# The delta rule's chunks and its output norm as one written-out stage, with two kinds of masked factors made by GpSimd

## The chip, the cores and the metric

One Trainium2 chip, one of its cores. The metric is the device time of one execution of the whole program in microseconds (us), the median of several runs. The engines are named as in the profile: PE is TensorE (PEld its weight loads), DVE is VectorE, ACT is ScalarE, POOL is GpSimd, SP the queue that issues the DMAs.

## What is computed

The program is two models in a row, on 512 tokens of width 1024 in float32: a block of differential attention, a state-space scan and a mixture of 64 experts, and then two layers, each of which mixes tokens in three ways (a delta rule with decay, a retention and a latent attention) before a gated feed-forward. The change is in the delta rule of these two layers. Its reference, cut to the recurrence and the norm after it (4 heads of 64):

```python
def step(state, inp):
    rt, kt, vt, wt, kkt, at = inp
    sa = jnp.einsum('bhvk,bhk->bhv', state, -kkt)
    state = (state * wt[:, :, None, :] + sa[..., None] * (kkt * at)[:, :, None, :]
             + vt[..., None] * kt[:, :, None, :])
    return state, jnp.einsum('bhvk,bhk->bhv', state, rt)
...
mean = jnp.mean(y, axis=-1, keepdims=True)
var = jnp.mean(jnp.square(y - mean), axis=-1, keepdims=True)
y = ((y - mean) * lax.rsqrt(var + RW_GN_EPS)).reshape(B, S, RW_DIM) * gn_w + gn_b
bonus = jnp.sum(r_h * k_h * r_k, axis=-1, keepdims=True) * v_h
y = (y + bonus.reshape(B, S, RW_DIM)) * g
```

## The kernel before

The program is a row of stages. Each stage is one block of five instruction streams, in the order in which they are written, which hand work to each other by semaphores; all engines meet at a barrier at its end. Nothing of one stage runs beside another.

The recurrence is done in chunks of 64 tokens. A tile `t` (there are NT = 4) holds two chunks on its 128 partitions and the 4 heads side by side, so that most tiles are 128 x 512. `stage_rwkv_chunks` has these steps:

- **Products** (L2915 to L2931 on PE, L3031 to L3043 on DVE, L3009 to L3013 on ACT). For each `t`, five products of 4 matmuls with a drain after each. DVE multiplies each by a mask from PSUM into SBUF (LT, Ti, MT, RB, RK) and then makes the first factors: `Ti = ident - Ti` (L3040), `TT = ident - LT * level0` (L3041, L3043). Six transposes per `t` go to ACT.
- **Inversion** (L2933 to L2956, L3014 to L3018, L3045 to L3061). Five levels in a hardware loop (`Fori`), each over the 4 tiles, that is 20 units `u`. For a unit DVE makes the masked factor `Lm = LT * level mask` (L3050), PE does `first`, 4 matmuls of Lm and Ti (L2952), ACT copies the result to X (L3018), PE does `second`, 4 matmuls to update Ti (L2942) and 4 to update TT (L2943), and DVE subtracts them (L3059, L3060). A float32 matmul is two passes in the trace, so a unit has 8 + 16 passes. On PE, `second` of a tile follows `first` of the next; `first` of every tile waits for `t_new` of the whole level before (L2949), and the factor of the next level is made after the last update of this one.
- **Mixed values and weighing** (L2958 to L2971): 4 matmuls of MT and the values per tile, 4 of TT and AM per tile, all after the last level; DVE copies the result into TW.
- **Parts** (L2973 to L2990). For each `t` 12 matmuls (the "front": G and y) and then 24 small ones of 64 x 64 (the "back": H and Z), one drain. Then DVE takes all of them (L3070 to L3081: one subtraction, one copy, 8 small instructions for H, 2 copies for Z). PE waits for `gh` of this tile before it begins the next (L2976).
- **States** (L2992 to L2996, L3083): 7 steps in a chain, PE then DVE. **Outputs** (L2998 to L3005, L3086): 4 tiles, PE then DVE.

`stage_rwkv_out` (L3095) is the norm of y over each head, on DVE alone but for one square root on ACT: 13 instructions, 10 of them over all 1024 columns, with a drain after each. `second_layer` calls both (L3173 to L3176) between `stage_mix` and `stage_ffn`, once in each layer.

Of the kernel before, what the change touches and what calls it, by code (L numbers as in the profile page):

```python
# [17 lines left out]
ds = bass.ds  # L18
# [2862 lines left out]
def stage_rwkv_chunks(k, l, out, eb, vt, y, spent):  # L2881

# [9 lines left out]
    W4 = HH * P  # L2892
    with ExitStack() as ctx:
# [10 lines left out]
        S = k.sb(f"rc{l}_S", [P, 8, 2, CH], F32, ctx)  # L2904
        bk = k.banks(ctx, 8, f"rc{l}_bk")
        lane = lambda h: slice(64 * (h % 2), 64 * (h % 2) + 64)
        pair = lambda p: (2 * (p % 3), 2 * (p % 3) + 1)
        s_ = {n: k.sem(f"rc{l}_" + n) for n in ("prod", "masked", "turned", "tok_taken", "lm", "x_mm", "x_sb", "y_mm", "t_new", "mv", "am", "tw_mm", "tw",
                                               "gh_mm", "gh", "s_mm", "s_new", "yo_mm", "yo_taken", "zero")}
        with nc.Block() as block:  # L2910
            @block.tensor
            def _(pe):
                pe.sem_inc(s_["y_mm"], 2)

                for t in range(NT):  # L2915
                    sl = slice(t * P, (t + 1) * P)
                    for n, (lhs, rhs) in enumerate(((B_, A_), (A_, B_), (K_, A_), (B_, R_), (K_, R_))):
                        if 5 * t + n >= 3:
                            pe.wait_ge(s_["masked"], 5 * t + n - 2)
                        for h in range(HH):  # L2920

                            o = bk[pair(5 * t + n)[h % 2]][:, (h // 2) * P:(h // 2 + 1) * P]
                            ins = pe.matmul(o, lhs[lane(h), h // 2, sl], rhs[lane(h), h // 2, sl], start=True, stop=True)
                        pe.drain().then_inc(s_["prod"], 1)
                    if t:
                        pe.wait_ge(s_["tok_taken"], 2 * t)
                    for n, src in enumerate((A_, Be, Ke)):
                        for b in range(2):
                            o = n * RW + b * P
                            ins = pe.transpose(bk[6 + o // 512][:, o % 512:o % 512 + P], src[:, b, sl], k.c("ident"))  # L2930
                    ins.then_inc(s_["turned"], 1)  # L2931

                pe.wait_ge(s_["masked"], 5 * NT)  # L2933
                with pe.Fori(0, 5) as lv:
                    def second(t):

                        u = lv * 4 + t
                        pe.wait_ge(s_["x_sb"], u + 1)
                        pe.wait_ge(s_["t_new"], u + 1)
                        for h in range(HH):  # L2940
                            hs = slice(h * P, (h + 1) * P)
                            pe.matmul(bk[2 + t % 2][:, hs], TT[:, t, h, :], X[t % 2][:, hs], start=True, stop=True)  # L2942
                            ins = pe.matmul(bk[4 + t % 2][:, hs], X[t % 2][:, hs], TT[:, t, h, :], start=True, stop=True)  # L2943
                        ins.then_inc(s_["y_mm"], 1)

                    for t in range(NT):
                        u = lv * 4 + t
                        pe.wait_ge(s_["lm"], u + 1)
                        pe.wait_ge(s_["t_new"], lv * 4 + 2)  # L2949
                        for h in range(HH):  # L2950
                            hs = slice(h * P, (h + 1) * P)
                            ins = pe.matmul(bk[t % 2][:, hs], Lm[t % 2][:, hs], Ti[:, t, h, :], start=True, stop=True)  # L2952
                        ins.then_inc(s_["x_mm"], 1)
                        if t:
                            second(t - 1)
                    second(NT - 1)  # L2956

                pe.wait_ge(s_["t_new"], 2 + 5 * NT)  # L2958
                for t in range(NT):
                    if t >= 2:  # L2960
                        pe.wait_ge(s_["am"], t - 1)
                    for h in range(HH):
                        ins = pe.matmul(bk[t % 2][:, h * 64:h * 64 + 64], MT[:, t, h, :], vt[:, t, h * 64:h * 64 + 64], start=True, stop=True)
                    ins.then_inc(s_["mv"], 1)
                for t in range(NT):
                    pe.wait_ge(s_["am"], t + 1)
                    if t >= 2:
                        pe.wait_ge(s_["tw"], t - 1)
                    for h in range(HH):
                        ins = pe.matmul(bk[2 + t % 2][:, h * P:(h + 1) * P], TT[:, t, h, :], AM[:, t, h, :], start=True, stop=True)  # L2970
                    ins.then_inc(s_["tw_mm"], 1)  # L2971

                for t in range(NT):  # L2973
                    pe.wait_ge(s_["tw"], t + 1)
                    if t:
                        pe.wait_ge(s_["gh"], t)  # L2976
# [15 lines left out]
                for c in range(7):  # L2992
                    pe.wait_ge(s_["s_new"], c + 1)
                    for h in range(HH):
                        ins = pe.matmul(bk[c % 2][lane(h), (h // 2) * 64:(h // 2) * 64 + 64], H[lane(h), h // 2, c, :], S[lane(h), c, h // 2, :], start=True, stop=True)
# [506 lines left out]
```

## Time and profile before

| | us |
|---|---|
| runs of the program | 3936.82, 3932.77, 3932.19 (median 3932.77) |
| profiled execution | 3927.36 |
| its span in the profile | 3925.5 |
| PE, DVE, ACT, POOL busy in the span | 3311.0, 1511.0, 1098.5, 175.8 |
| the two stages of layer 0 | 2347.8 to 2537.4 on the span's clock |
| the two stages of layer 1 | 3281.0 to 3472.3 |

A row of the timeline gives start, duration, engine, line, operation, output<-inputs, shape and count, and in brackets how long the engine was idle before it and for whom. PEq and DVEq are the engines' own sequencers: a wait for a drain of PE or DVE. A duration of a row with several instructions is from the first start to the last end. The granted clock of PE has two levels, 2.4 GHz (1.00) and 1.2 GHz (0.50).

### The profile page before, as it was taken

How to read it: one execution, taken by the hardware profiler on the slowest of the kernel's cores; microseconds unless marked ns; L12 is line 12 of the kernel's file. 1: busy time of each engine (PE TensorE's matmuls, PEld its weight loads, DVE VectorE, ACT ScalarE, POOL GpSimd, SP SyncE). 2: the span in 40 equal slices, each digit the busy share in tenths (PEclk: the TensorE clock that was granted, in tenths of full speed). 3: DMA queues.
4: the chain of work that ended last, by engine and by line, in shares of the span. 5: the costliest groups of instructions: out<-in, count | busy, mean ns of one | idle time of the engine just before them, and what ended most of it. 6: DMA issues, size and time to landing. Idle time of an engine off the chain costs nothing. (4 is left out here: it accounts for less than half of the span.)

```text
span 3925.5 us, 42592 instructions
## 1 busy us (share of the span) xinstructions
PE 3311.0 (84%) x16382; PEld 2352.5 (60%) x16382; DVE 1511.0 (38%) x2518; ACT 1098.5 (28%) x1853; POOL 175.8 (4%) x204
## 2 busy tenths in 40 slices
PE   5998999999677788787849888599998988769997
PEld 3776877777333233333317557478886746757886
DVE  4772566643410001000034565433323665443332
ACT  3672666642100000000013341132223242123221
POOL 0000222200000000000000000000000000000000
PEclk9999999999799999989979978599999986779999
DMA  3223222223899999999943100123323100022332
GB/s 93 64 66 67 71 65 65 65 70 95 327 427 426 426 426 425 416 415 421 415 184 93 28 1 1 35 78 97 99 97 83 49 11 1 1 78 81 97 102 76
DMA packets 355521, 601.90 MB, mean 153 GB/s; under 512 B 72288, under 2 KB 306560, under 8 KB 330624
## 3 DMA queue, kind: packets, MB, share of 16 engines
q1 hardware_dynamic: 346112, 590.85, 41.2%
q0 software_dynamic: 9216, 8.42, 0.6%
q8 instruction: 128, 2.10, 0.2%
q14 instruction: 65, 0.53, 0.0%
HBM read 603.40 MB, written 20.97 MB: 159 GB/s over the span
## 5 line engine op out<-in xcount | busy, mean ns | idle before, releaser
L1729 PE MATMUL ex_up<-ex_W,ex_XT 128*64 128x512 f32 x1024 | 262.2, 670 | 97.0 <-DMA ex_W<-in_w_expert_up_dram 97.0
L226 ACT ACTIVATE f_hi<-f_raw 128x1024 fp32r<-128x1024 f32 x148 | 156.8, 1059 | 576.0 <-PE ff_bk L286 548.8
L1729 PE MATMUL ex_gp<-ex_W,ex_XT 128*64 128x512 f32 x1024 | 237.8, 618 | 59.7 <-DMA ex_W<-in_w_expert_gate_dram 58.3
L235 DVE TENSOR_TENSOR f_lo<-f_raw,f_hi 128x1024 fp32r<-128x1024 f32 x148 | 181.1, 1224 | 257.9 <-ACT f_hi L226 257.7
L284 PE MATMUL ff_bk<-h_a_hi,f_hi 128*128 128x512 f32 x704 | 275.9, 392 | 2.8 <-DVE h_a_lo L3361 2.8
L285 PE MATMUL ff_bk<-h_a_lo,f_hi 128*128 128x512 f32 x704 | 275.3, 391 | 0.0
L286 PE MATMUL ff_bk<-h_a_hi,f_lo 128*128 128x512 f32 x704 | 275.1, 391 | 0.0
L1772 DVE TENSOR_TENSOR ex_hid<-ex_sg,ex_up 128x512 f32<-128x512 f32 x32 | 22.0, 688 | 614.9 <-PE ex_up L1729 614.9
L1758 PE MATMUL ex_yp<-ex_W,ex_hT 128*64 128x512 f32 x1024 | 226.8, 594 | 35.1 <-DMA ex_W<-in_w_expert_down_dram 20.3
L1729 PEld LDWEIGHTS ex_up<-ex_W,ex_XT 128*64 128x64 f32 x1024 | 92.3, 153 | 266.3 <-issue 266.3
L1729 PEld LDWEIGHTS ex_gp<-ex_W,ex_XT 128*64 128x64 f32 x1024 | 87.6, 142 | 209.0 <-issue 207.2
L235 DVE TENSOR_TENSOR b_lo<-b_raw,b_hi 128x1024 fp32r<-128x1024 f32 (+1 forms) x121 | 147.9, 1234 | 124.0 <-ACT b_hi L226 123.8
L284 PE MATMUL ff_bk<-f_hi,fT_hi 128*128 128x512 f32 x480 | 187.6, 391 | 0.0
L285 PE MATMUL ff_bk<-f_lo,fT_hi 128*128 128x512 f32 x480 | 187.1, 390 | 0.0
L286 PE MATMUL ff_bk<-f_hi,fT_lo 128*128 128x512 f32 x480 | 187.0, 390 | 0.0
L1758 PEld LDWEIGHTS ex_yp<-ex_W,ex_hT 128*64 128x64 f32 x1024 | 84.7, 137 | 155.2 <-issue 155.2
L284 PE MATMUL ss_acc<-h_x_hi,b_hi 128*128 128x512 f32 x320 | 131.9, 412 | 29.3 <-DVE b_lo L235 29.3
L226 ACT ACTIVATE b_hi<-b_raw 128x1024 fp32r<-128x1024 f32 (+1 forms) x121 | 125.7, 1048 | 109.9 <-PE mg_bk L286 64.9
L284 PEld LDWEIGHTS ff_bk<-h_a_hi,f_hi 128*128 128x128 f32 x704 | 133.0, 189 | 31.6 <-DVE h_a_lo L3361 3.6
L286 PEld LDWEIGHTS ff_bk<-h_a_hi,f_lo 128*128 128x128 f32 x704 | 133.0, 189 | 27.8
L285 PEld LDWEIGHTS ff_bk<-h_a_lo,f_hi 128*128 128x128 f32 x704 | 133.1, 189 | 27.5
L286 PE MATMUL ss_acc<-h_x_hi,b_lo 128*128 128x512 f32 x320 | 128.6, 402 | 0.0
(606 smaller groups left out, 6620.4 us busy)
## 6 DMA issues: line engine op xcount, KB each, us to landing
ex_W<-in_w_expert_gate_dram SPq DMA_DIRECT2D x64, 2048.0 KB, 29.4
ex_W<-in_w_expert_up_dram SPq DMA_DIRECT2D x64, 2048.0 KB, 29.6
ex_W<-in_w_expert_down_dram SPq DMA_DIRECT2D x64, 2048.0 KB, 28.9
b_raw<-in_w_in_dram SPq DMA_DIRECT2D x88, 512.0 KB, 3.9
f_raw<-in_w_gate_up_dram SPq DMA_DIRECT2D x88, 512.0 KB, 3.8
f_raw<-in_w_down_dram SPq DMA_DIRECT2D x44, 512.0 KB, 3.5
m_raw<-in_w_in_dram SPq DMA_DIRECT2D x40, 512.0 KB, 4.0
b_raw<-in_w_branch_ssd_dram SPq DMA_DIRECT2D x16, 512.0 KB, 4.0
```

The costliest lines, as they stand in the source:

```text
L226: a.activation(self.hi[n % self.SLOTS][:, at], self.raw[n % self.RAW][:, at], ACT.Copy).then_inc(self.cast, 1)
L235: v.tensor_tensor(self.lo[i][:, at], self.raw[n % self.RAW][:, at], self.hi[i][:, at].bitcast(F32), ALU.subtract).then_inc(self.split_done, 1)
L284: pe.matmul(out, a[0], b[0], start=first, stop=False)
L285: pe.matmul(out, a[0], b[1], start=False, stop=False)
L286: return pe.matmul(out, a[1], b[0], start=False, stop=last)
L1729: ins = pe.matmul(ps[part[e], :], XT[b][:, q, part[e]], row_view(slots[e], KD)[:, q, :], start=(q == 0), stop=(q == KD - 1))
L1758: ins = pe.matmul(y_ps[s][part[e], :], hT[:, q, part[e]], row_view(slots[e], HT)[:, q, s * 512:(s + 1) * 512], start=(q == 0), stop=(q == ...
L1772: v.tensor_tensor(hid[:], sg[:], u_ps[:], ALU.mult).then_inc(hid_ready, 1)
```

## The change

The two stages become one, `stage_delta`. What it does:

- The level loop is written out over 20 units. `first(u)` waits for the factor `lm` of this unit and for `t_new` of the same tile one level before. In the last level the update of Ti is left out.
- GpSimd makes the first TT factors (two instructions per tile) and all 20 `Lm`. It then makes `eye` and `H = pc * eye`, and the norm's `gate` and `gt` with four instructions of 128 x 1024.
- Mixed values run on PE behind units 0 to 3, weighing behind the last units. ACT takes TW, y and Z in place of DVE.
- In the parts, front and back have their own drain and semaphores, and nothing waits for the taking of the same tile. States 1 to 3 and the outputs are placed between and behind the parts, the norm is done per tile, between the later states. State 0 is a copy.
- y, gate, sq and the norm's rows lie in memory left by an earlier stage. The norm's rows are loaded at the stage's begin.

The diff, cut to its core:

```diff
-                with pe.Fori(0, 5) as lv:
...
+            @block.gpsimd
+            def _(g):
+                for t in range(NT):
+                    g.wait_ge(masked, 5 * t + 1)
+                    g.tensor_tensor(TT[:, t], LT[:, t], over("rw_level0"), ALU.mult)
+                    g.drain()
+                    g.tensor_tensor(TT[:, t], over("ident"), TT[:, t], ALU.subtract).then_inc(tt_ready, 1)
+                for u in range(LEVELS * NT):
+                    t = u % NT
+                    if u >= 2:
+                        g.wait_ge(x_mm, u - 1)
+                    g.tensor_tensor(Lm[t % 2][:].rearrange("p (h n) -> p h n", h=HH), LT[:, t], over(f"rw_level{u // NT + 1}"), ALU.mult).then_inc(lm, 1)
...
+            @block.tensor
+                def first(u):
+                    t = u % NT
+                    pe.wait_ge(lm, u + 1)
+                    if u < NT:
+                        pe.wait_ge(ti_ready, t + 1)
+                    else:
+                        pe.wait_ge(t_new, u - NT + 1)
+                    if u >= 2:
+                        pe.wait_ge(x_sb, u - 1)
...
+                def parts(t):
+                    pe.wait_ge(tw, t + 1)
                     if t:
+                        pe.wait_ge(front_v, t)
+                        pe.wait_ge(front_a, t)
...
+                    pe.drain().then_inc(front_mm, 1)
+                    if t:
+                        pe.wait_ge(back_v, t)
+                        pe.wait_ge(back_a, t)
...
+                first(0)
+                for u in range(1, LEVELS * NT):
+                    first(u)
+                    second(u - 1)
+                    if u <= NT:
+                        mixed_values(u - 1)
+                    if u >= LAST + 2:
+                        weigh(u - LAST - 2)
+                second(LEVELS * NT - 1)
+                weigh(NT - 2)
+                weigh(NT - 1)
+                parts(0)
+                parts(1)
+                state(1)
+                parts(2)
+                state(2)
+                parts(3)
+                state(3)
+                outputs(0)
+                state(4)
+                outputs(1)
+                state(5)
+                outputs(2)
+                state(6)
+                outputs(3)
...
+            @block.vector
+                def spread(t):
+                    v.drain()
+                    do(v.tensor_reduce, mean[:, t, :], heads(y, t), AX, ALU.add)
+                    do(v.tensor_scalar, mean[:, t, :], mean[:, t, :], 1.0 / 64, None, ALU.mult)
+                    do(v.tensor_tensor, heads(y, t), heads(y, t), each(mean, t), ALU.subtract)
+                    do(v.tensor_tensor, sq[:, t, :], y[:, t, :], y[:, t, :], ALU.mult)
+                    do(v.tensor_reduce, var[:, t, :], heads(sq, t), AX, ALU.add)
+                    v.tensor_scalar(var[:, t, :], var[:, t, :], 1.0 / 64, 64e-5, ALU.mult, ALU.add).then_inc(var_ready, 1)
+                def normalize(t):
+                    v.wait_ge(root_ready, t + 1)
+                    do(v.reciprocal, var[:, t, :], var[:, t, :])
+                    do(v.tensor_tensor, heads(y, t), heads(y, t), each(var, t), ALU.mult)
+                    if t == 0:
+                        v.wait_ge(gates_ready, 1)
+                    do(v.tensor_tensor, y[:, t, :], y[:, t, :], gt[:, t, :], ALU.mult)
+                    v.tensor_tensor(mix[:, t, 0:RW], y[:, t, :], gate[:, t, :], ALU.add)
...
+                for u in range(LEVELS * NT):
+                    update(u)
+                take_front(0)
...
+                take_back(3)
+                add_state(3)
+                add_outputs(0)
+                add_state(4)
+                spread(0)
+                add_outputs(1)
+                add_state(5)
+                normalize(0)
+                add_outputs(2)
+                add_state(6)
+                spread(1)
+                spread(2)
+                normalize(1)
+                add_outputs(3)
+                spread(3)
+                normalize(2)
+                normalize(3)
```

## Rows read from the trace of the kernel before

**Rows 1.** Windows of the two stages: us, PE, PEld, DVE, ACT, POOL busy, clock, DMA, GB/s.

```profile
2347.80:2381.80 34.00, 30.42 (x184) 23.28 (x184) 22.97 (x53) 3.49 (x8) 0.00 (x0) 0.50 0.00 1
2381.80:2462.40 80.60, 67.24 (x544) 66.07 (x544) 41.35 (x66) 15.00 (x28) 0.00 (x0) 0.93 0.00 0
2462.40:2471.20 8.80, 5.60 (x73) 4.47 (x72) 3.79 (x14) 0.00 (x0) 0.00 (x0) 1.00 0.01 2
2471.20:2507.60 36.40, 28.34 (x216) 22.49 (x216) 7.14 (x26) 0.00 (x0) 0.00 (x0) 0.50 0.00 1
2507.60:2537.40 29.80, 7.66 (x120) 5.61 (x120) 20.22 (x40) 1.50 (x2) 0.00 (x0) 0.50 0.03 9
...
3313.40:3397.30 83.90, 70.64 (x544) 69.50 (x544) 41.36 (x66) 15.02 (x28) 0.00 (x0) 0.90 0.00 0
```

**Rows 2.** Timeline, end of the products and begin of the inversion, both layers.

```profile
2373.37 0.75 DVE L3035 TENSOR_TENSOR rc_LT<-rc_bk,more_consts 128x256 f32<-128x256 f32 x2
...
2379.51 0.63 PE L2930 MATMUL rc_bk<-consts,rw_Ke 128*128 128x128 f32 x2
...
2382.71 3.57 PE L2952 MATMUL rc_bk<-rc_Ti,rc_Lm 128*128 128x128 f32 x16 [2.57 <-DVE rc_Lm L3050]
...
3310.68 0.38 PE L2930 MATMUL rc_bk<-consts,rw_Ke 128*128 128x128 f32 x2
...
3314.30 1.52 PE L2952 MATMUL rc_bk<-rc_Ti,rc_Lm 128*128 128x128 f32 x5 [3.24 <-DVE rc_Lm L3050]
```

**Rows 3.** Timeline inside the inversion, two units and the next level's begin.

```profile
2388.11 0.69 DVE L3059 TENSOR_TENSOR rc_Ti<-rc_Ti,rc_bk 128x512 f32<-128x512 f32 x1 [2.60 <-PE rc_bk L2943]
...
2390.79 0.69 DVE L3059 TENSOR_TENSOR rc_Ti<-rc_Ti,rc_bk 128x512 f32<-128x512 f32 x1 [0.51 <-PE rc_bk L2943]
...
2397.98 2.05 PE L2952 MATMUL rc_bk<-rc_Ti,rc_Lm 128*128 128x128 f32 x16 [2.76 <-DVE rc_Lm L3050]
```

**Rows 4.** Timeline, mixed values and weighing of layer 0.

```profile
2454.79 3.79 PE L2963 MATMUL rc_bk<-rw_vt,rc_MT 128*128 128x64 f32 x32 [1.41 <-DVEq L3061]
2458.41 4.10 PE L2970 MATMUL rc_bk<-rc_AM,rc_TT 128*128 128x128 f32 x32
```

**Rows 5.** GpSimd's instructions of two lines, min/median/max in ns.

```profile
L883 POOL TENSOR_TENSOR ss_rows<-consts,ss_adt x32: 1040/1250/1485, 412.6 to 789.5; 128x512 f32<-128x512 f32 x32
...
L871 POOL TENSOR_TENSOR ss_xdt<-ss_xs,ss_dt x32: 607/611/1590, 416.1 to 759.1; 128x256 f32<-128x256 f32 x32
```

**Rows 6.** Timeline of the parts: PE's first matmul, DVE's first taking.

```profile
2462.44 0.43 PE L2979 MATMUL rc_bk<-rc_RB,rc_LT 128*64 128x128 f32 x2
...
2468.06 0.42 DVE L3070 TENSOR_TENSOR rkv<-rw_R,rc_bk 128x256 f32<-128x256 f32 x1 [4.75 <-PEq L2990]
...
2471.74 0.66 PE L2979 MATMUL rc_bk<-rc_RB,rc_LT 128*64 128x128 f32 x2 [3.74 <-DVEq L3081]
...
2481.24 0.42 DVE L3070 TENSOR_TENSOR rkv<-rw_R,rc_bk 128x256 f32<-128x256 f32 x1 [9.68 <-PEq L2990]
...
2507.62 0.42 DVE L3070 TENSOR_TENSOR rkv<-rw_R,rc_bk 128x256 f32<-128x256 f32 x1 [9.69 <-PEq L2990]
...
3397.33 0.43 PE L2979 MATMUL rc_bk<-rc_RB,rc_LT 128*64 128x128 f32 x2
```

**Rows 7.** Timeline of DVE behind the parts of layer 0.

```profile
2513.17 0.29 DVE L3085 TENSOR_TENSOR rc_S<-rc_bk,rkv 128x128 f32<-128x128 f32 x1 [0.81 <-PEq L2996]
...
2521.47 0.48 DVE L3090 TENSOR_TENSOR rw_y<-rw_y,rc_bk 128x128 f32<-128x128 f32 x2 [0.33 <-PEq L3005]
...
2523.61 1.22 DVE L3118 TENSOR_REDUCE ro_0mean<-rw_y 128x16 f32<-128x1024 f32 x1 [0.84 <-PEq L134]
2524.91 0.17 DVE L3118 TENSOR_SCALAR ro_0mean<-ro_0mean 128x16 f32<-128x16 f32 x1
2525.16 1.23 DVE L3118 TENSOR_TENSOR rw_y<-rw_y,ro_0mean 128x1024 f32<-128x1024 f32 x1
...
2536.15 1.23 DVE L3138 TENSOR_TENSOR mix<-rw_y,rw_gt 128x1024 f32<-128x1024 f32 x1
```

More of the change, by code:

```diff
@@ L2904, in stage_rwkv_chunks @@
         S = k.sb(f"rc{l}_S", [P, 8, 2, CH], F32, ctx)
+        y, gate, sq, wb = (k.over(f"rc{l}_{n}", [P, NT, RW], F32, at + i * 4 * NT * RW) for i, n in enumerate(("y", "gate", "sq", "wb")))
+        eye = k.sb(f"rc{l}_eye", [P, CH], F32, ctx)
+        mean, var = k.sb(f"rc{l}_mean", [P, NT, HH], F32, ctx), k.sb(f"rc{l}_var", [P, NT, HH], F32, ctx)
         bk = k.banks(ctx, 8, f"rc{l}_bk")
@@ L2933, in _ @@
-                pe.wait_ge(s_["masked"], 5 * NT)
-                with pe.Fori(0, 5) as lv:
[L2935 to L2971, printed above, removed]
@@ new lines, in second @@
+                def second(u):
+                    t = u % NT
+                    pe.wait_ge(x_sb, u + 1)
+                    if u < NT:
+                        pe.wait_ge(tt_ready, t + 1)
+                    if u >= 2:
+                        pe.wait_ge(t_new, u - 1)
+                    for h in range(HH):
+                        hs = sl(h)
+                        if u < LAST:
+                            pe.matmul(bk[2 + t % 2][:, hs], TT[:, t, h, :], X[t % 2][:, hs], start=True, stop=True)
+                        ins = pe.matmul(bk[4 + t % 2][:, hs], X[t % 2][:, hs], TT[:, t, h, :], start=True, stop=True)
+                    ins.then_inc(y_mm, 1)
@@ L2997, in _, with state @@
-                pe.wait_ge(s_["s_new"], 8)
-                for t in range(NT):
+                            pe.matmul(bk[5 + c][lane(h), o:o + 64], tok[rows, t, 1, f], TW[rows, t, h, 64:128], start=False, stop=True)
+                    pe.drain().then_inc(back_mm, 1)
+                def state(c):
+                    pe.wait_ge(back_v, c // 2 + 1)
+                    pe.wait_ge(back_a, c // 2 + 1)
+                    if c >= 2:
+                        pe.wait_ge(s_new, c - 1)
+                    else:
+                        pe.wait_ge(tw, NT)
+                    for h in range(HH):
+                        pe.matmul(bk[2][lane(h), (h // 2) * 64:(h // 2) * 64 + 64], H[lane(h), h // 2, c, :], S[lane(h), c, h // 2, :], start=True, stop=True)
+                    pe.drain().then_inc(s_mm, 1)
@@ new lines, in take_parts, with root @@
+                def take_parts(t):
+                    a.wait_ge(front_mm, t + 1)
+                    a.activation(y[:, t, :], bk[7][:, 0:RW], ACT.Copy).then_inc(front_a, 1)
+                    a.wait_ge(back_mm, t + 1)
+                    for c in range(2):
+                        where = S[:, 1] if t == 0 and c == 0 else Z[:, :, 2 * t + c, :]
+                        ins = a.activation(where, half(5 + c), ACT.Copy)
+                    ins.then_inc(back_a, 1)
+                def root(t):
+                    a.wait_ge(var_ready, t + 1)
+                    a.activation(var[:, t, :], var[:, t, :], ACT.Sqrt).then_inc(root_ready, 1)
@@ L3021, in _ @@
-                    a.wait_ge(s_["mv"], t + 1)
-                    a.activation(AM[:, t, :, 64:128], bk[t % 2][:, 0:RW].rearrange("p (h n) -> p h n", h=HH), ACT.Copy)
-                    a.drain().then_inc(s_["am"], 1)
+                    take_parts(t)
+                for t in range(NT):
+                    root(t)
             @block.vector
             def _(v):
-                over = lambda name: k.c(name).rearrange("p (a n) -> p a n", a=1).broadcast_to([P, HH, P])
-                v3 = lambda b: bk[b][:].rearrange("p (h n) -> p h n", h=HH)
```

283 lines of the change are left out of this document (145 added, 138 removed).

## The prediction

> **What bounds the kernel now.** I read first which stretch of the span the change touches. The table of windows gives it: layer 0 spends 34.0 us in the products, 80.6 in the inversion with mixed values and weighing, 45.2 in the parts and 29.8 behind them, 189.6 in all; layer 1 is the same but for 83.9 us in the inversion [rows 1]. No engine works outside these two stages meanwhile, so a microsecond saved here is one saved in the program. Then I read who waits for whom. In the inversion PE is the bound: between two updates of DVE lie 2.68 us (2390.79 - 2388.11), which is 24 passes of PE at 0.112 us. Only at a level's begin does PE stand still, 2.76 us until the new factor [rows 3], and the granted clock, 1.00 inside a level, has a mean of 0.93 and 0.90 [rows 1]. In the parts PE and DVE take turns: DVE waits 9.68 us, PE 3.74 [rows 6]. Behind the parts PE is busy 7.7 us of 29.8, DVE 20.2: a chain of small steps and then the norm on DVE [rows 1].
>
> **Begin of the inversion.** In the products the drains between the groups stay, and DVE, which loses two of its three 128x512 instructions per tile, wasn't the bound there; I let the 34 us stand (between 0 and 1.4 us less per tile if I am wrong, since two instructions of 0.69 us go). After the last transpose (2379.51 + 0.63 = 2380.1) PE now waits until 2382.71; in layer 1 from 3311.1 to 3314.30 [rows 2]. GpSimd needs the last LT, 2374.1 [rows 2], plus two instructions for TT and one for the factor at 1.25 us each [rows 5], so it has the factor at 2378. PE starts right behind the transposes: 2.5 and 3.1 us saved.
>
> **Inversion.** 20 `first` of 8 passes, 16 `second` of 16, 4 of 8 (the last level without Ti), 32 of mixed values and 32 of weighing: 512 passes. At 0.112 us that is 57.3 us. The rows of the two added kinds are no dearer: 32 passes in 3.79 and 4.10 us, with their ends in it [rows 4]. The first passes of a dense stretch run at the lower level: 16 in 3.57 us [rows 2] against 16 in 2.05 at a later level [rows 3], so 1.5 us for that stretch; I take 2 us in layer 0 and 1 in layer 1, which now comes without a pause out of its products (bounds 0 and 3). Two short waits at the end, for the last update and for TW, get 0.4. So 59.7 and 58.7 us, against 79.7 (2382.71 to 2462.44) and 83.0 (3314.30 to 3397.33) [rows 2, 6]: 20.0 and 24.3 us saved.
>
> What must keep up: `t_new` of a tile is needed three units after it starts to be made, over 5 us for two instructions of 0.69. ACT copies a unit in 0.6 us of its 2.68. GpSimd has a factor of 1.25 us to make per 2.68, and from the end of `first(u-2)` to `first(u)` PE has 40 passes, 4.5 us. The instruction itself, masks times LT over 128x512, is not in the trace. The nearest row is L883, which has the same shape, a broadcast operand too and 1.04 to 1.49 us; the dearest is the longest of L871, 1.59 us for half the columns [rows 5], so 3.18 is the upper end. I take 1.25: it is the median of the same shape, and hidden.
>
> H and the four gate instructions on GpSimd (five of 128x1024, 2.5 us each by twice L883, 12.5 us) run beside weighing and parts; only H is needed at once, at the end of the first part, some 8 us after the last factor. Without that cover it would cost 2.5 us. TW and the copies move to ACT at the same sizes and are idle time there.
>
> **Parts.** One part takes PE and its drain 5.6 us at the upper level (2462.44 to 2468.06) and 9.5 at the lower (2471.74 to 2481.24); then PE stands for DVE, 3.7 us [rows 6]. Now the takings of a front lie beside the back and those of a back beside the next front, each under 1.5 us, since the eight small instructions for H are two. The wait goes. The front gets a drain: a state step shows 0.81 us for 8 passes, a drain and the way to DVE [rows 7], so the drain alone is between 0 and 0.8, and I take 0.2, because most of that is the passes and because only the last matmul's end is waited for. Two state steps on PE between the parts cost 0.6 us each (bounds 0.4 and 0.8). With all at the upper level: 4 x 5.8 + 1.2 = 24.4 us; with only the first, as now, 5.8 + 3 x 9.7 + 1.6 = 36.5. Today the clock is 1.00 through the first part and in the wait behind it, and 0.50 in everything after that wait [rows 1]. The wait is what ends it and it is gone, but new drains and two state steps are little work, and the rows also show that three later stretches of 9.5 us without a gap did not bring the upper level back. I take one of the four parts at the lower level: 24.4 + 3.8 = 28.2 us. Saved: 45.2 - 28.2 = 17.0 in each layer.
>
> **Behind the parts.** Counted from PE's last part. Now: 29.8 us. New: state(3) ends at 0.8, outputs(0) at 1.65, DVE adds it until 2.25, state(4) is added at 2.8. From then DVE is the bound. A norm instruction of 256 columns costs 0.42 (the same width in rows 6) and 0.07 for the drain, as the 1.22 us one starts the next after 1.30; a small one costs 0.25 [rows 7]. A `spread` is 4 x 0.49 + 2 x 0.25 = 2.5 us, a `normalize` 0.25 + 3 x 0.49 = 1.7. Four of each, three additions of outputs at 0.49 and two of states at 0.29 make 18.9 us [rows 7], and the end is at 21.7; I take 21.5, since the last has no drain. PE's chain hides in it (1.1 us a state). The square root is asked for long before it is used. One barrier of 0.84 us [rows 7] is in the difference. Saved: 8.3 us in each layer.
>
> **Sum.** Layer 0: 2.5 + 20.0 + 17.0 + 8.3 = 47.8. Layer 1: 3.1 + 24.3 + 17.0 + 8.3 = 52.7. Together 100.5 us, so the profiled execution would go from 3927.4 to 3826.9. The median of the runs is 5.4 us above that execution; against it the forecast is 3932.8 - 100.5 = 3832 us.
>
> **Rivals.**
> 1. *The parts stay at the lower clock.* For it: once down, no part of today got it back. Against it: it fell only in a 3.7 us pause that is gone. Each layer loses 8.3 us more: 3849 us.
> 2. *GpSimd sets the pace of the inversion.* It decides once a factor takes more than 2.68 us. At 3.18 us each of 20 units is 0.5 longer, and the last level's saving (3.6 us a layer) is not had: some 14 us a layer, 3860 us. For it are the long ones among the 32 of L871 (1.59 beside a median of 0.61) [rows 5]; against it the longest 128x512 row, 1.49. The Trainium skill ("SBUF — State Buffer", Who interferes with whom) says that a DVE instruction with two SBUF inputs and a GpSimd instruction that reads SBUF hold each other up for a whole instruction. In the inversion DVE's updates take one operand from PSUM, so by that rule they leave GpSimd alone, and it speaks against this rival; the rule would bite between `spread` and the gates, which do not meet by the times above. The skill's "GPSIMD Engine Reference", Engine selection, advises VectorE for elementwise work as about twice as fast; the rows agree (1.25 against 0.69 us), but here it is GpSimd's idle time that pays.
> 3. *The level's pause is not removed.* If it came from the chain of data and not from the order of the work, four pauses of 2.76 us per layer would stay: 3832 + 22 = 3854 us. Against it: `t_new` of tile 0 is there when PE still has three tiles of the level before it.
> 4. *Slower than before.* The place is again the factor: GpSimd makes one only after PE has freed its buffer, and everything on PE is behind it. It must eat the whole gain: 100.5 us over 40 units is 2.5 us each on top of 2.68, so it decides at 5.2 us a factor with its signals. At 5.7 us the time is 3953. No row of GpSimd of this size is above 1.49.
>
> **Chances.** Forecast 0.68 (its own range 3818 to 3845, from the ramp and from no or two parts at the lower level), rival 1 0.14, rival 2 0.07, rival 3 0.06, rival 4 0.03; 0.02 for a gain and a loss that cancel. Range 3813 to 3860: the low end has all parts at the upper level (7.6), no ramp (3), and the states and outputs at the upper clock, and the high end takes in rivals 1 to 3. A change under 0.2% (8 us) can't be told from none: faster 0.95, same 0.02, slower 0.03.
>
> **What would show it.** Right: DVE's updates every 2.68 us over all 20 units with no gap at a level's begin; PE's clock 1.00 from the first level on; GpSimd's factor rows about 1.25 us and waiting for PE; front and back of the parts without a DVE wait, and a part 5.8 us; DVE busy without a gap from state 4 to the end. Wrong: PE waiting for `Lm` in each unit (rival 2) or in every fourth (3), a part near 9.7 us with the clock at 0.50 (1), or the norm starting much later than the first outputs.

## The result, and the profile after

| | kernel before | changed kernel |
|---|---|---|
| median of the runs, us | 3932.48 (3928.35 to 3936.82, 4 runs) | 3811.87 (3809.06 to 3816.76, 4 runs) |
| ratio, 95% interval | | 0.9694 [0.9678, 0.9711] |
| profiled execution, us | 3927.36 | 3816.76 |
| its span, us | 3925.5 | 3814.9 |
| stage of layer 0, layer 1, us | 189.6, 191.3 | 136.1, 134.4 |

The change saved 120.6 us by the medians; 3832 was forecast, in a range from 3813 to 3860. The sign came as forecast, and the mechanism too but for the clock of the parts; the size did not: the time lies 1.1 us below the range's low end and 20 below the forecast.

First the windows of both stages after the change (us; busy time of PE, weight load, DVE, ACT, GpSimd; granted clock; DMA share; GB/s). They show the products, the inversion (in two pieces in layer 0), the parts (in two pieces), and what is behind them; then layer 1. The cuts are where the next part of the work begins on PE, but for the end of the parts, which is the end of DVE's last taking. They answer to [rows 1].

```profile
2348.50:2380.50 32.00, 30.21 (x185) 23.43 (x186) 17.89 (x45) 2.62 (x6) 12.60 (x10) 0.50 0.04 9
2380.50:2399.40 18.90, 18.90 (x163) 18.90 (x163) 5.29 (x9) 7.21 (x16) 7.56 (x6) 0.96 0.01 2
2399.40:2438.70 39.30, 39.30 (x352) 39.16 (x350) 18.17 (x28) 10.23 (x20) 22.45 (x17) 1.00 0.01 1
2438.70:2444.50 5.80, 5.68 (x74) 4.46 (x72) 0.42 (x1) 1.04 (x3) 3.91 (x2) 1.00 0.01 3
2444.50:2464.50 20.00, 17.95 (x240) 14.42 (x240) 3.79 (x13) 3.00 (x12) 0.00 (x0) 1.00 0.00 1
2464.50:2484.60 20.10, 4.03 (x92) 3.00 (x88) 16.21 (x52) 2.04 (x5) 0.00 (x0) 0.57 0.00 1
3226.10:3256.20 30.10, 28.15 (x184) 21.45 (x184) 17.54 (x45) 2.74 (x7) 11.41 (x10) 0.56 0.03 10
3256.20:3314.50 58.30, 57.75 (x512) 57.40 (x512) 23.82 (x37) 17.33 (x36) 31.72 (x24) 1.00 0.00 1
3314.50:3340.30 25.80, 23.56 (x313) 18.88 (x312) 4.21 (x14) 4.02 (x15) 3.86 (x2) 1.00 0.01 2
```

In the inversion PE is now busy all but without a gap (39.30 of 39.30 us, 57.75 of 58.30), 512 passes where there were 544. The parts run at a granted clock of 1.00 from first to last, and only behind them does it fall. Each term of the sum has its line here.

The timeline of the inversion, with the start, the duration and in brackets the idle time before and what ended it. The rows answer to [rows 2, 3]:

```profile
2377.33 2.50 POOL L2932 TENSOR_TENSOR rc_Lm<-rc_LT,more_consts 128x512 f32<-128x512 f32 x2
...
2380.47 2.76 PE L2960 MATMUL rc_bk<-rc_Ti,rc_Lm 128*128 128x128 f32 x16
...
2400.34 1.27 POOL L2932 TENSOR_TENSOR rc_Lm<-rc_LT,more_consts 128x512 f32<-128x512 f32 x1 [1.41 <-PE rc_bk L2960]
2402.09 0.69 DVE L3146 TENSOR_TENSOR rc_Ti<-rc_Ti,rc_bk 128x512 f32<-128x512 f32 x1 [1.40 <-PE rc_bk L2974]
...
2404.76 0.69 DVE L3146 TENSOR_TENSOR rc_Ti<-rc_Ti,rc_bk 128x512 f32<-128x512 f32 x1 [1.39 <-PE rc_bk L2974]
...
3257.88 1.16 PE L2960 MATMUL rc_bk<-rc_Ti,rc_Lm 128*128 128x128 f32 x8 [0.50 <-POOL rc_Lm L2932]
```

PE begins right behind the transposes (the last starts at 2380.04), with no wait of 2.57 us for the factor. The updates lie 2.67 us apart. Each factor takes GpSimd 1.27 us, after which it waits 1.41 for PE. Once, at the begin of layer 1's inversion, PE waits half a microsecond for it.

The timeline of the parts, for [rows 6]: PE's first matmul, then each later part's first, and DVE's takings.

```profile
2438.75 0.43 PE L3004 MATMUL rc_bk<-rc_RB,rc_LT 128*64 128x128 f32 x2
...
2442.68 0.42 DVE L3151 TENSOR_TENSOR rkv<-rw_R,rc_bk 128x256 f32<-128x256 f32 x1 [5.07 <-PEq L3007]
...
2444.69 0.40 PE L3004 MATMUL rc_bk<-rc_RB,rc_LT 128*64 128x128 f32 x2 [0.23 <-issue]
...
2451.40 0.40 PE L3004 MATMUL rc_bk<-rc_RB,rc_LT 128*64 128x128 f32 x2 [0.23 <-issue]
...
2458.12 0.40 PE L3004 MATMUL rc_bk<-rc_RB,rc_LT 128*64 128x128 f32 x2 [0.23 <-issue]
...
2463.98 0.49 DVE L3158 TENSOR_TENSOR rkv<-rkv,rc_bk 128x128 f32<-128x128 f32 x2 [1.54 <-PEq L3019]
```

The 3.74 us before the second part are gone; 0.23 us behind a drain is all that is left. From one part's first matmul to the next one's it is 5.94 us, or 6.71 with a state step in it.

### The profile page after: what moved, and what is told of

It reads as the page before. It is cut to its first block and busy times, and to the rows that moved or that the text cites. A ratio compares the mean times of both kernels' runs of the same rounds, so it can differ in the third digit from the quotient of the medians.

```text
span 3814.9 us, 42208 instructions
## 1 busy us (share of the span) xinstructions
PE 3270.0 (86%) x16302; PEld 2316.5 (61%) x16302; DVE 1443.0 (38%) x2418; ACT 1111.4 (29%) x1899; POOL 269.3 (7%) x272
## 5 line engine op out<-in xcount | busy, mean ns | idle before, releaser
L1729 PE MATMUL ex_gp<-ex_W,ex_XT 128*64 128x512 f32 x1024 | 246.4, 636 | 61.8 <-DMA ex_W<-in_w_expert_gate_dram 60.4
```

The source lines that it names most:

```text
L1729: ins = pe.matmul(ps[part[e], :], XT[b][:, q, part[e]], row_view(slots[e], KD)[:, q, :], start=(q == 0), stop=(q == KD - 1))
```

## What the executions themselves scatter by

The sum was made against one execution of the kernel before, so the first question was whether that one is typical. I profiled the kernel before twice more and the changed kernel once more.

> The kernel before, unchanged, profiled once more. The profiled execution of before was 5 to 7 us under the median of its runs, and my sum was made against it. Theory: the difference is TensorE's clock, which rises in some executions and not in others in the same stretch of work; then the two stages (189.6 and 191.3 us in the first profile) or the strips between them take 3 to 7 us more in this one and the granted clock differs there. Rival: all stretches repeat within 1 us and the difference lies outside the span.

> The kernel before once more, for a third profile: by the theory its stage lengths scatter by some us with the clock granted in the products (0.50 throughout in the first profile) and in the inversion's pauses; by the rival they repeat within 1 us.

> The changed kernel once more. Theory 1 (the gain is what the two profiles show inside the delta stage, 53.5 us in layer 0 and 56.9 in layer 1, and the other 10 us of the medians' difference are scatter of the rest of the program): the saving over five rounds is 106 to 118 us, and windows of the delta stage repeat within 0.5 us while the rest of the span moves by several us between profiles. Theory 2 (the change also speeds the stages outside the delta stage): the saving stays at 120 us and the rest of the span is shorter than before in the new profile too.

Measured: the two executions of the kernel before took 3934.74 and 3935.44 us (spans 3932.9 and 3933.6). The changed kernel again: 3812.43 us (3809.58 to 3818.49, 5 runs), ratio 0.9695 [0.9682, 0.9709], span 3812.7. Both kernels are cut at the same places in this table, and as in the forecast's sum the parts end where DVE begins to take the last of them (in the windows above, where it ends, half a microsecond later):

| us | before, three profiles | changed, two profiles |
|---|---|---|
| span up to the first stage | 2347.9, 2353.2, 2353.7 | 2348.4, 2349.2 |
| products, layers 0 + 1 | 68.1, 68.1, 68.0 | 62.1, 60.2 |
| inversion | 162.7, 163.8, 165.1 | 116.8, 116.1 |
| parts | 90.3, 90.2, 90.2 | 50.5, 50.4 |
| behind the parts | 59.7, 59.5, 59.6 | 41.3, 41.3 |
| between the two stages | 743.6, 743.8, 743.7 | 741.4, 740.7 |
| behind the second stage | 453.2, 454.3, 453.3 | 454.5, 454.8 |

The parts and what is behind them repeat within 0.2 us. The first profile of before was short by 5.3 to 5.8 us ahead of the first stage, in code that the change leaves alone, and by 1.1 to 2.4 in the inversion. So "within 1 us everywhere" was wrong, and the difference lies inside the span; but most of it isn't in the two stages, where the theory looked first. With the means of these profiles the account closes: 6.9 us in the products, 47.4 in the inversion, 39.8 in the parts, 18.3 behind them, 4.4 in the rest, together 116.9, against 120.6 by the medians.

The products differ for another reason. The same stretch from ten to fifteen microseconds into the products of layer 0 in the changed kernel, from its repetition and from a kernel below whose work is the same to the instruction up to there (`parts_wait`). The window of the changed kernel:

```profile
2358.50:2363.50 5.00, 4.64 (x32) 3.48 (x31) 2.77 (x9) 0.00 (x0) 2.54 (x2) 0.50 0.00 0
```

Windows of its repetition:

```profile
2359.30:2364.30 5.00, 4.64 (x32) 3.48 (x31) 2.77 (x9) 0.00 (x0) 2.53 (x2) 0.50 0.00 0
2364.30:2369.30 5.00, 4.65 (x44) 3.57 (x44) 3.70 (x10) 0.87 (x2) 1.86 (x2) 0.82 0.00 0
...
2374.30:2379.30 5.00, 4.73 (x30) 3.87 (x31) 3.24 (x9) 0.00 (x0) 4.35 (x4) 0.50 0.00 0
```

And that of `parts_wait`:

```profile
2361.80:2366.80 5.00, 4.56 (x52) 3.46 (x50) 4.33 (x12) 0.87 (x2) 2.54 (x2) 0.99 0.00 0
```

The granted clock is 0.50 throughout in the first, rises for about seven microseconds and falls again in the second, and is 1.00 from the tenth microsecond on in the third. The products take 31.9, 30.0 and 24.1 us. Where the clock is 0.50, PE is busy 4.6 to 4.8 us of five in all of them; the gaps are those behind the drains. The instructions are the same in all three; what decides between them is not shown. Over twelve such stretches, in these three profiles and in three more of kernels below that change only the level's wait, the parts or the norm, they took 24.1 to 31.9 us: a scatter of up to 8 us per layer out of one and the same code.

## The inversion: what GpSimd and the order are worth

**The factor back on DVE.** DVE makes TT and the factors, these two units ahead, and the order on PE stays as changed:

```diff
-                    g.tensor_tensor(Lm[t % 2][:].rearrange("p (h n) -> p h n", h=HH), LT[:, t], over(f"rw_level{u // NT + 1}"), ALU.mult).then_inc(lm, 1)
+                    v.tensor_tensor(Lm[t % 2][:].rearrange("p (h n) -> p h n", h=HH), LT[:, t], over(f"rw_level{u // NT + 1}"), ALU.mult).then_inc(lm, 1)
...
+                factor(0)
+                factor(1)
                 for u in range(LEVELS * NT):
+                    if u + 2 < LEVELS * NT:
+                        factor(u + 2)
                     update(u)
```

> The written-out stage, but DVE makes the first TT factors and all masked factors, as before the change; GpSimd keeps H and the gates. Theory 1 (PE is the bound of the inversion, and who makes the factor is nearly free): DVE has 0.69 + 1.37 = 2.06 us of work per unit of 2.68, so units stay 2.68 us and only the start of the inversion is later, by 2 to 3 us a layer: 3 to 8 us slower than the changed kernel in all. Theory 2 (GpSimd's share is what made the gain): updates and factors queue on DVE, a unit takes 3.2 us or more, 20 us or more slower than the changed kernel.

Measured: 3818.14 us (3812.20 to 3824.03, 5 runs), ratio 0.9709 [0.9692, 0.9725]; the interval overlaps that of the changed kernel. In the profile the inversion takes 59.6 and 60.5 us instead of 58.5 and 58.3, and in both layers PE waits 2.98 us for its begin, where the changed kernel does not wait or 0.22 us:

```profile
2381.59 2.84 PE L2951 MATMUL rc_bk<-rc_Ti,rc_Lm 128*128 128x128 f32 x16 [2.98 <-issue]
```

That later begin does not show in the stage's length (134.6 and 136.2 us against 136.1 and 134.4), because the products happened to get a higher clock in this profile (0.71 and 0.67 against 0.50 and 0.56). By the medians the move to GpSimd is worth 5.7 us over both layers, as theory 1 had it (3 to 8), though inside the scatter. DVE had room: three instructions of 0.69 us per 2.68.

The rest of the inversion's 47 us is the written-out order and the passes left out, and a good part of it is clock. In the first profile of before PE stands still for 24.9 us of the 162.7 (79.7 less 67.24 and 83.0 less 70.63), and its 1088 passes take 137.9 us, where at the 0.114 us of the changed kernel they would take 124.0. So, as an estimate: 24 us of pauses, 14 of lower clock and 7 for the 64 passes left out. That clock fell behind some of the pauses at a level's begin and not behind others of the same length: in layer 0 the 16 passes behind the four of them took 2.05, 2.45, 3.57 and 2.05 us, and here is the second:

```profile
2411.76 2.45 PE L2952 MATMUL rc_bk<-rc_Ti,rc_Lm 128*128 128x128 f32 x16 [2.74 <-DVE rc_Lm L3050]
...
2414.00:2417.00 3.00, 3.00 (x17) 3.00 (x17) 0.00 (x0) 0.60 (x1) 0.00 (x0) 0.56 0.00 0
```

**A level waits for the level before it.**

```diff
-                        pe.wait_ge(t_new, u - NT + 1)
+                        pe.wait_ge(t_new, u // NT * NT)
...
-                    first(u)
-                    second(u - 1)
+                    if u % NT == 0:
+                        second(u - 1)
+                        first(u)
+                    else:
+                        first(u)
+                        second(u - 1)
```

> The changed kernel, but the first products of a level wait until every tile of the level before is updated, and so stand behind its last second products. Theory 1 (the pause at a level's begin came from this order, not from the chain of data): four pauses of 1.7 to 2.5 us come back in each layer, and the clock may fall after some: 14 to 30 us slower than the changed kernel. Theory 2 (the gain came from writing the loop out, without branches and register waits): under 5 us slower.

Measured: 3828.90 us (3827.67 to 3831.46, 5 runs), ratio 0.9738 [0.9724, 0.9751], 16.5 us above the changed kernel. The timeline of its PE shows the pause at a level's begin again; it comes four times in a layer:

```profile
2394.20 1.13 PE L2960 MATMUL rc_bk<-rc_Ti,rc_Lm 128*128 128x128 f32 x8 [1.42 <-issue]
...
2407.47 2.02 PE L2960 MATMUL rc_bk<-rc_Ti,rc_Lm 128*128 128x128 f32 x16 [1.43 <-issue]
```

The inversion takes 64.5 and 65.1 us, 6.0 and 6.8 more; four pauses of 1.43 are 5.7. So it is the order that removes the pause, which rival 3 doubted. Its price was put too high: 1.43 us each and not the 2.76 of [rows 3], since the factors are already made. The clock stays at 1.00 over each of these eight pauses. Theory 2, by which this kernel would be under 5 us slower, is out.

**The factor two and three times.** GpSimd makes each factor twice, or three times, with a drain between, to see from where on it sets the pace.

```diff
+                    for n in range(2):   # 3 in the other kernel
+                        g.drain()
-                    g.tensor_tensor(Lm[t % 2][:].rearrange("p (h n) -> p h n", h=HH), LT[:, t], over(f"rw_level{u // NT + 1}"), ALU.mult).then_inc(lm, 1)
+                        ins = g.tensor_tensor(Lm[t % 2][:].rearrange("p (h n) -> p h n", h=HH), LT[:, t], over(f"rw_level{u // NT + 1}"), ALU.mult)
+                    ins.then_inc(lm, 1)
```

> GpSimd makes each masked factor twice (2.5 to 2.7 us a unit with a drain). Theory 1 (hidden as long as a factor takes less than PE's 2.68 us a unit, and 4.5 us from release to use): up to 5 us slower in all. Theory 2 (the factor is on the path with its signals already): a unit takes 1.3 us longer, 50 us slower in all.

> GpSimd makes each masked factor three times (3.9 to 4.1 us a unit). It sets the pace: a unit takes that time in place of 2.68 and the last level's saving is not had, 20 units x 1.4 to 1.8 us plus 3 us: 60 to 75 us slower than the changed kernel in all, still faster than the kernel before. If instead it is slower by less than 20 us, the pace is not set by the factor at all.

Measured: 3825.05 us (3824.31 to 3825.27, 4 runs), 0.9729 [0.9712, 0.9746], and 3873.02 us (3872.89 to 3879.43, 4 runs), 0.9857 [0.9838, 0.9876]. GpSimd in the kernel with two:

```profile
2399.10 2.69 POOL L2934 TENSOR_TENSOR rc_Lm<-rc_LT,more_consts 128x512 f32<-128x512 f32 x2 [0.16 <-issue]
2401.95 2.69 POOL L2934 TENSOR_TENSOR rc_Lm<-rc_LT,more_consts 128x512 f32<-128x512 f32 x2 [0.16 <-issue]
```

GpSimd and PE in the kernel with three:

```profile
2397.70 4.09 POOL L2934 TENSOR_TENSOR rc_Lm<-rc_LT,more_consts 128x512 f32<-128x512 f32 x3 [0.16 <-issue]
2401.85 1.16 PE L2963 MATMUL rc_bk<-rc_Ti,rc_Lm 128*128 128x128 f32 x8 [1.21 <-POOL rc_Lm L2934]
2401.95 4.09 POOL L2934 TENSOR_TENSOR rc_Lm<-rc_LT,more_consts 128x512 f32<-128x512 f32 x3 [0.16 <-issue]
```

A factor every 2.85 us, with no idle time left on GpSimd, makes the inversion 63.9 us (5.6 more); every 4.25 us it makes it 86.7 (28.4 more, where 20 units of 1.57 us are 31.4). PE also begins it later in both kernels, in layer 0 after a wait of 2.61 and 4.02 us. By the medians they are 13 and 61 us slower than the changed kernel. The "up to 5 us" for two held only for a factor under 2.68 us, and with its drains it took 2.85; the 60 to 75 for three came true. So GpSimd decides already at 2.85 us, just above PE's 2.68, as rival 2 said. The line through the two points of the inversion gives 16 us a layer for each microsecond of the period, and so an estimate of 11 a layer at 3.18 us, where 14 were forecast. The kernel with the factor three times is still 1.4% faster than the one before: rival 4 needed more than that.

## The parts: the step that failed

Two kernels put DVE's takings back between the parts. In the first each front waits for the takings of the back before it; in the second DVE also does five multiplications of 128x512 before it takes each of the first three backs, which makes PE's waits 4.63, 3.70 and 3.70 us in layer 0, about the 3.74 of [rows 6].

```diff
                         pe.wait_ge(front_v, t)
                         pe.wait_ge(front_a, t)
+                        pe.wait_ge(back_v, t)
+                        pe.wait_ge(back_a, t)
...
+                    if t < NT - 1:          # the second kernel only
+                        for n in range(5):
+                            v.tensor_tensor(X[0][:], X[1][:], X[1][:], ALU.mult)
+                            v.drain()
```

> The changed kernel, but the front of a part waits until DVE and ACT have taken the back of the part before. Theory 1 (the parts gain twice, the pause itself and the upper clock that survives without it; a pause under 1 us doesn't cost the clock): three pauses of 0.7 us, clock 1.00 through all parts, 2 to 3 us slower a layer. Theory 2 (any pause here costs the clock): parts from the second on at 0.50 and 9.7 us each, about 12 us slower a layer.

> As the last, and DVE does five more 128x512 instructions on unused data before it takes a back (0.76 us each with their drains), so that the pause is about 4.4 us, as long as before the change. Theory 1 (the pause ends the upper clock): parts 2 to 4 at 0.50 and 9.7 us each, so 13 us of pauses and 11 us of clock a layer, 45 to 50 us slower than the changed kernel in all. Theory 2 (the clock in the parts follows their own work and not the pause): 26 us slower in all, clock 1.00.

Measured: 3813.51 us (3812.95 to 3819.09, 4 runs), 0.9704 [0.9686, 0.9723], and 3855.93 us (3852.42 to 3862.88, 4 runs), 0.9814 [0.9794, 0.9834]. The windows of the parts in layer 0 with the short wait:

```profile
2435.00:2440.50 5.50, 4.78 (x68) 3.79 (x67) 0.91 (x3) 0.83 (x3) 3.02 (x2) 1.00 0.01 3
2440.50:2461.50 21.00, 18.51 (x256) 14.77 (x256) 3.59 (x12) 3.37 (x10) 0.00 (x0) 1.00 0.00 1
```

And with the long one: DVE's five instructions and PE's first matmul behind them, then windows of the end of the first part, the wait, and what follows it:

```profile
2437.17 3.76 DVE L3161 TENSOR_TENSOR rc_X<-rc_X 128x512 f32<-128x512 f32 x5 [1.41 <-PEq L3021]
...
2441.74 0.66 PE L3006 MATMUL rc_bk<-rc_RB,rc_LT 128*64 128x128 f32 x2 [4.63 <-DVE rkv L3164]
...
2434.00:2437.40 3.40, 3.03 (x57) 2.52 (x56) 0.65 (x2) 0.61 (x3) 1.41 (x1) 1.00 0.02 5
2437.40:2441.40 4.00, 0.00 (x0) 0.00 (x0) 3.63 (x7) 0.21 (x2) 0.00 (x0) 0.97 0.00 0
2441.40:2445.00 3.60, 3.26 (x12) 2.44 (x12) 0.09 (x1) 0.00 (x0) 0.00 (x0) 0.50 0.00 0
2445.00:2455.00 10.00, 6.92 (x69) 5.60 (x68) 3.60 (x6) 0.83 (x3) 0.00 (x0) 0.50 0.00 0
2455.00:2465.00 10.00, 8.68 (x64) 6.88 (x66) 1.39 (x5) 0.38 (x1) 0.00 (x0) 0.50 0.01 2
```

The short wait is one of 0.80 and two of 0.34 us, where 0.7 each were expected; it costs 0.8 us a layer and not 2 to 3, and leaves the clock alone. The long one puts a pause of over four microseconds behind the first part, and from its end on the granted clock is 0.50 for all that follows, three parts long. The parts take 49.3 us, 22.8 more than with the short wait. PE's three pauses grew by 10.6 us together (12.0 against 1.5); the other 12.2 are three parts and two state steps at the lower level, where [rows 6] put a part at 3.9 us more (9.5 against 5.6), 11.7 for three. So pauses of this length took the clock, here as in the kernel before. Both have such a pause before each later part too, so no run shows whether one alone would do it for long. Against the changed kernel the median is 44 us higher, 45 to 50 were expected. The drains and the two state steps with their 0.23 us gaps never took the clock: in all 20 stretches of parts in the ten profiles of kernels with the changed parts and without the long wait the granted clock is 1.00, and they take 25.7 to 26.5 us from the first matmul to the end of the last taking.

## Behind the parts, and the products

**The norm undivided.** Instead of four `spread` and four `normalize` of a quarter each between the outputs, one set of ten instructions behind the last output (seven over all 1024 columns, three small ones), and one square root:

```diff
-                spread(0)
...
-                normalize(3)
+                do(v.tensor_reduce, flat(mean), hv(y[:]), AX, ALU.add)
+                do(v.tensor_scalar, flat(mean), flat(mean), 1.0 / 64, None, ALU.mult)
+                do(v.tensor_tensor, hv(y[:]), hv(y[:]), bc(mean), ALU.subtract)
...
+                v.tensor_tensor(mix[:, :, 0:RW], y[:], gate[:], ALU.add)
```

> The changed kernel, but the norm is one set of 10 instructions over all four tiles behind the last output, in place of four sets between the states. Theory 1 (behind the parts DVE is the bound, and each instruction has a fixed share that four sets pay four times): states and outputs end about 7 us after the parts, then 7 x 1.30 + 3 x 0.25 us = 9.9 us: 17 us in place of 20.6, so 3.5 us a layer and 7 us in all faster than the changed kernel. Theory 2 (laying the norm between the states is what gained): 5 us or more slower a layer.

Measured: 3807.80 us (3800.61 to 3816.10, 5 runs), ratio 0.9679 [0.9663, 0.9696]. By the medians 4.6 us are gained, inside the scatter; the profile is clearer, because this stretch repeats: 16.8 and 16.6 us instead of 20.1. DVE in the changed kernel:

```profile
2466.43 0.42 DVE L3178 TENSOR_REDUCE rc_mean<-rc_y 128x4 f32<-128x256 f32 x1
2466.93 0.17 DVE L3178 TENSOR_SCALAR rc_mean<-rc_mean 128x4 f32<-128x4 f32 x1
...
2484.20 0.43 DVE L3198 TENSOR_TENSOR mix<-rc_y,rc_gate 128x256 f32<-128x256 f32 x1
```

DVE with the undivided norm, in whose profile the parts end 0.9 us earlier:

```profile
2469.75 0.48 DVE L3170 TENSOR_TENSOR rc_y<-rc_y,rc_bk 128x128 f32<-128x128 f32 x2 [0.93 <-PEq L3045]
2470.33 1.22 DVE L3178 TENSOR_REDUCE rc_mean<-rc_y 128x16 f32<-128x1024 f32 x1
...
2479.16 1.23 DVE L3245 TENSOR_TENSOR mix<-rc_y,rc_gate 128x1024 f32<-128x1024 f32 x1
```

Counted from the end of the parts, the norm that was cut up begins 4.8 us earlier (2466.43 against 2470.33 + 0.9) and ends 3.3 later. A quarter costs 0.49 us with its drain, four of them 1.96 where a whole one takes 1.30, and the small ones come four times. Lying beside PE's chain for 4.8 us does not pay for that. Theory 1 had 3.5 us a layer, and 3.3 to 3.5 were measured.

**Products without drains.** The last two matmuls of a group signal in place of a drain behind it; this goes beyond the change, after the clock's scatter above.

```diff
                             ins = pe.matmul(o, lhs[lane(h), h // 2, sl(t)], rhs[lane(h), h // 2, sl(t)], start=True, stop=True)
-                        pe.drain().then_inc(prod, 1)
+                            if h >= 2:
+                                ins.then_inc(prod, 1)
...
-                        v.wait_ge(prod, 5 * t + n + 1)
+                        v.wait_ge(prod, 10 * t + 2 * n + 2)
```

> The changed kernel with the 20 drains behind the groups of products left out; the last two matmuls of a group signal instead. Products take 24.1 to 32 us in the profiles so far, by the clock granted in them. Theory: PE's short gaps behind the drains (4.7 of 5 us busy) keep the clock from rising; without them it rises in every execution and the products take 23 to 25 us in both layers: 3800 us. Rival: it rises or not whatever these gaps are; then at most the gaps' 1 to 2 us a layer go: 3809 us. A third: DVE bounds the products at the upper clock, so nothing is gained where the clock is 1.00 already (24 us stays 24).

> The changed kernel without the drains in the products and with the norm as ten whole-width instructions behind the last output (3.4 us less behind the parts of each layer in its own profile). If the two add: 6.8 us below no_drain, 3794 to 3803 us, the fastest so far. Rival: the earlier rise in the products costs later clock, and the gain is 4.6 us or less against no_drain.

Measured: `no_drain` 3795.32 us (3793.28 to 3798.39, 5 runs), ratio 0.9660 [0.9647, 0.9674]. `both`, which has the whole-width norm too, 3789.28 us (3783.54 to 3791.81, 5 runs), ratio 0.9641 [0.9628, 0.9654], the fastest here: by the ratios 0.5% of the time before, about 21 us, below the changed kernel. The windows of the products and of the inversion's begin in `no_drain`:

```profile
2350.50:2352.50 2.00, 1.99 (x18) 2.00 (x20) 0.89 (x3) 0.00 (x0) 0.00 (x0) 0.50 0.18 51
2352.50:2354.50 2.00, 2.00 (x27) 1.88 (x25) 1.80 (x7) 0.00 (x0) 1.74 (x2) 0.73 0.66 90
2354.50:2359.50 5.00, 4.72 (x56) 3.94 (x58) 4.90 (x15) 1.07 (x3) 3.06 (x3) 1.00 0.01 1
...
2364.50:2369.30 4.80, 2.59 (x30) 1.92 (x27) 4.71 (x12) 0.87 (x2) 3.85 (x4) 1.00 0.00 0
2369.30:2374.00 4.70, 4.19 (x22) 4.01 (x23) 0.46 (x1) 1.50 (x3) 3.71 (x3) 0.64 0.00 0
```

Its timeline at the inversion's begin:

```profile
2367.95 4.16 POOL L2932 TENSOR_TENSOR rc_Lm<-rc_LT,more_consts 128x512 f32<-128x512 f32 x3
...
2369.31 1.13 PE L2960 MATMUL rc_bk<-rc_Ti,rc_Lm 128*128 128x128 f32 x8 [1.84 <-issue]
...
2370.94 2.08 PE L2960 MATMUL rc_bk<-rc_Ti,rc_Lm 128*128 128x128 f32 x8 [0.50 <-POOL rc_Lm L2932]
```

PE is busy without a gap at first, and the clock is at 1.00 four microseconds in. The products take 18.8 and 20.1 us (18.8 and 19.0 in `both`), with a mean clock of 0.85 to 0.92: the theory held in all four stretches, where it was at most 0.79 in the twelve with drains. Its 23 to 25 us were too much. The third possibility, that DVE would hold them at 24 us, was wrong; but DVE is the bound now, busy 4.90 us of five, a group every 0.66 us where with drains at the same clock it was 0.80. What is late next also shows: PE, busy for only 2.59 of the last 4.8 us of the products, waits 1.84 and 0.50 us at the inversion's begin. Its first matmul starts when GpSimd's first factor of the row above (1.27 us from 2367.95) is there, so GpSimd is now late here. The clock falls once more (0.64 in the window behind), and the inversion takes 59.7 us in layer 0 (58.3 in layer 1; 59.8 and 59.6 in `both`). So of the 10 to 13 us a layer that the products lose against the two profiles of the changed kernel, 17 us over both layers arrive in the median. The undivided norm gives 6.0 us on top by the medians and 8.1 by the profiles (16.1 and 16.0 us against twice 20.1), where 6.8 were expected: the two edits add, and the time is below the 3794 to 3803 only because `no_drain` itself was faster than its 3800.

## Why the forecast was right in kind and wrong in size

The forecast's error of 20.1 us is made up of 1.3 at the begin of the inversion, 3.1 in it, 5.8 in the parts, 1.7 behind them, and 8.1 outside the four terms.

- **Begin of the inversion: right.** 5.6 us forecast for both layers, 6.9 measured. "I let the 34 us stand" was fair for DVE's removed instructions (34.8 became 31.9 with the wait gone), but what sets the products is which clock they get, and that differed from one execution to the next.
- **Inversion: right, a little small.** 44.3 forecast, 47.4 measured, with 58.3 us for 512 passes where 59.7 and 58.7 were taken. At 58.3, a pass is 0.114 us on the mean, where 0.112 were taken; 1.2 of the 3.1 us are the first profile's shorter inversions. The ramp in layer 0 cost less than the 2 us I took, since the 16 first passes were 2.76 us, not 3.57.
- **Parts: the step that failed.** "I take one of the four parts at the lower level" put them at 28.2 us; they took 25.2, all at 1.00, 5.8 us over both layers. It is the largest single term of the error. Without that choice the same sum says 24.4. The paragraph had the reason at hand (today's clock falls in the 3.7 us wait and the wait goes) and set against it "new drains and two state steps are little work". `parts_long` shows that pauses of that length take the level, `parts_wait` and the drains that short ones don't. The third remark, that 9.5 us stretches at the lower level did not bring the upper one back, was true and beside the point: here it never left.
- **Behind the parts: right.** 16.6 forecast, 18.3 measured. Where no drain stands between two of DVE's instructions the next begins before the one ahead has ended (one of 0.17 us at 2468.67, the addition at 2468.78); the sum had them end to end.
- **One profile for the whole: wrong.** The forecast took the saving off the median, and the saving from a single profile, as if all outside the two stages stayed as it is. That profile was 5.3 to 5.8 us early before the first stage. By the means of the profiles 4.4 us are saved outside the terms: 2.8 before the first stage, by scatter, and 2.6 in the strip between the stages (743.6 to 743.8 us in three profiles before, 740.7 and 741.4 after), less 1.0 behind the second. That strip was left out of the sum. Most of its gain lies in the stage right behind: the first use of its weights comes 5.3 to 5.4 us after their transfer is issued in the three profiles before, and 3.6 and 4.0 after; why is not shown. The other 3.7 us are the difference between the means of the profiles (116.9) and of the medians (120.6).

None of the rivals occurred. Brought about on purpose, the clock lost in the parts (rival 1) costs 12.2 us a layer, where the sum's own figures give 12.1 for three parts (36.5 less 24.4; the 8.3 of the rival are counted from a forecast that has one part at the lower level already). The slow factor (2) costs 11 by the line above where it was 14, the level's pause (3) 6.4 where it was 11, and a factor of 4.25 us is not yet slower than before (4).

## What to carry to other kernels

Ask of every pause of TensorE how long it is before asking what follows it: here pauses of 4 us between the parts cost the upper clock in the three parts behind the first of them, ones of 2.7 us in dense work cost it for about three microseconds in some cases and not at all in others, and single ones of 0.23 to 1.43 us in dense work cost only themselves. Where a stretch stands at the lower clock with TensorE nearly always busy, look for drains between its groups: signalling from the last matmuls instead took 10 to 13 us a layer off that stretch here, and 17 us off the program. And before a sum is set against a profile, take more than one: what didn't change scattered by 5 us, nearly as much as the largest term of the error.

## What the runs showed of the hardware

- The granted clock of one and the same stretch of instructions (the products) was 0.50 throughout, up and down again, or 1.00 from the tenth microsecond on, in executions of kernels that are alike up to there; in the first ten microseconds, at 0.50, TensorE was busy for 4.7 of five us each time.
- Leaving out the drain behind a group of small matmuls gave 0.14 us at the same, upper clock (a group per 0.66 us instead of 0.80, with DVE then the bound), 2.8 us for the 20 groups of a layer. The rest of the 10 to 13 us by which the products of a layer got shorter was mostly the clock.
- GpSimd's product of two 128x512 operands is 1.27 us where DVE takes 0.69, and of 128x1024 1.90 or 2.35 us; DVE's updates, beside it in the inversion, stay at the 0.69 us of [rows 3]. The Trainium skill ("GPSIMD Engine Reference", Engine selection) advises VectorE as about twice as fast, which these rows bear out (1.8 times). Here the slower product cost nothing, since GpSimd still waited 1.41 us for PE after each.
